# Placing the moving operands of a two-block transformer kernel: other start addresses for the second block's activations and products

## The reference

```python
def swiglu(x, w_gate, w_up, w_down):
    return (jax.nn.silu(x @ w_gate) * (x @ w_up)) @ w_down
...
    for l in range(DEPTH):
        h = rmsnorm(x, ffn1_norm[l])
        x = x + 0.5 * swiglu_2(h, ffn1_w_gate[l], ffn1_w_up[l], ffn1_w_down[l])
        h = rmsnorm(x, mix_norm[l])
        p = h @ w_in[l]
        ...
        y = jnp.concatenate([y_pool, y_four, y_attn], axis=-1) @ w_out[l]
        x = x + y
        h = rmsnorm(x, ffn2_norm[l])
        x = x + 0.5 * swiglu_2(h, ffn2_w_gate[l], ffn2_w_up[l], ffn2_w_down[l])
    return rmsnorm(x, final_norm)
```

## Time and profile before

| | |
|---|---|
| median of 3 runs | 1993.99 us (1993.69 to 1995.05) |
| the profiled execution | 1994.2 us, span of its instructions 1992.4 us |
| mean granted TensorE clock | 0.999 |
| PE busy | 1976.9 us, 99% of the span, 16,150 matmuls |
| DVE, ACT, POOL busy | 1429.0 us (72%), 1019.4 us (51%), 152.7 us (8%) |
| the three lines of `three` | 84% of the chain that ended last |

### The profile page before, as it was taken

The page is one execution under the profiler, slowest core; times in us unless marked ns, Lnnn a source line. Parts: engine busy times, 40 slices in busy tenths (PEclk is TensorE's granted clock), DMA queues, the critical chain, the costliest instruction groups (busy, mean ns, idle before and its releaser), DMA issues.

```text
span 1992.4 us, 42293 instructions
## 1 busy us (share of the span) xinstructions
PE 1976.9 (99%) x16150; PEld 1936.5 (97%) x16150; DVE 1429.0 (72%) x2593; ACT 1019.4 (51%) x1525; POOL 152.7 (8%) x192
## 2 busy tenths in 40 slices
PE   9999999999999999999999999999999999999998
PEld 9999989999999999899999999999999999999998
DVE  6774887886688769888868775667756775667763
ACT  4433686554455447765446444564444443555443
POOL 0001122000100011210010000010000000100000
PEclk9999999999999999999999999999999999999999
DMA  7454423545454544245554664335454555435554
GB/s 258 172 203 165 170 86 128 190 168 196 157 182 175 188 150 164 86 174 193 184 188 152 223 220 179 128 146 192 179 215 165 190 201 193 148 125 180 189 208 150
DMA packets 46830, 346.66 MB, mean 174 GB/s; under 512 B 5344, under 2 KB 6416, under 8 KB 9232
## 3 DMA queue, kind: packets, MB, share of 16 engines
q1 hardware_dynamic: 44416, 335.63, 46.5%
q0 software_dynamic: 2320, 9.74, 1.5%
HBM read 344.29 MB, written 1.07 MB: 173 GB/s over the span
## 4 chain that ended last, share of the span: by engine, by line
PE 88%; DVE 6%; ACT 2%; DVEq 1%; issue 1%; DMA 0%; ACTq 0%; POOL 0%; SPq 0%
PE ps L589 28%; PE ps L591 28%; PE ps L590 28%; DVE w_lo L1909 2%; ACT w_hi L1235 1%; DVE cst L2378 0%; DVE pj L2357 0%; PE ps L1135 0%; DVE pj L2354 0%; ACT scratch L1586 0%; PE ps L1100 0%; DVE scratch L2323 0%; DMA raw<-in_w_up 0%; PE ps L925 0%; PE ps L936 0%
## 5 line engine op out<-in xcount | busy, mean ns | idle before, releaser
L1909 DVE TENSOR_TENSOR w_lo<-raw,w_hi 128x1024 fp32r<-128x1024 f32 (+1 forms) x582 | 748.7, 1313 | 167.4 <-ACT w_hi L1235 165.4
L1235 ACT ACTIVATE w_hi<-raw 128x1024 fp32r<-128x1024 f32 (+1 forms) x582 | 634.9, 1121 | 140.4 <-PE ps L591 126.5
L589 PE MATMUL ps<-x_hi,w_lo 128*128 128x256 f32 (+3 forms) x2416 | 693.0, 287 | 2.7 <-DVE x_lo L1996 1.4
L591 PE MATMUL ps<-x_hi,w_hi 128*128 128x256 f32 (+3 forms) x2416 | 685.5, 284 | 0.0
L590 PE MATMUL ps<-x_lo,w_hi 128*128 128x256 f32 (+3 forms) x2416 | 680.6, 282 | 0.0
L589 PEld LDWEIGHTS ps<-x_hi,w_lo 128*128 128x128 f32 x2416 | 454.6, 188 | 11.1 <-issue 5.9
L590 PEld LDWEIGHTS ps<-x_lo,w_hi 128*128 128x128 f32 x2416 | 455.4, 188 | 0.8
L591 PEld LDWEIGHTS ps<-x_hi,w_hi 128*128 128x128 f32 x2416 | 454.4, 188 | 0.0
L589 PE MATMUL ps<-hid_hi,w_lo 128*128 128x256 f32 (+1 forms) x1536 | 435.5, 284 | 0.7 <-DVE hid_lo L2107 0.4
L590 PE MATMUL ps<-hid_lo,w_hi 128*128 128x256 f32 (+1 forms) x1536 | 434.0, 283 | 0.0
L591 PE MATMUL ps<-hid_hi,w_hi 128*128 128x256 f32 (+1 forms) x1536 | 433.4, 282 | 0.0
(11 more groups left out here) (330 smaller groups left out, 1538.9 us busy)
## 6 DMA issues: line engine op xcount, KB each, us to landing
raw<-in_w_up SPq DMA_DIRECT2D x176, 1024.0 KB, 4.8
raw<-in_w_down SPq DMA_DIRECT2D x64, 1408.0 KB, 6.0
raw<-in_w_in SPq DMA_DIRECT2D x36, 1024.0 KB, 4.8
raw<-in_w_out SPq DMA_DIRECT2D x16, 1024.0 KB, 4.9
cst<-row_copy POOLq DMA_DIRECT2D x2, 1088.0 KB, 8.6
raw<-in_w_up SPq DMA_DIRECT2D x4, 512.0 KB, 6.8
cst<-in_consts POOLq DMA_DIRECT2D x1, 1537.5 KB, 6.5
prm<-in_prm POOLq DMA_DIRECT2D x2, 690.0 KB, 7.5
```

Of the source, the lines that this page charges most:

```text
L589: mm(dst, w_lo[:, j, cols], xa, start=first, stop=False)
L591: return mm(dst, w_hi[:, j, cols], xa, start=False, stop=last)
L1235: fn(w_hi[:, j, c], raw[:, j, c], ACT.Copy).then_inc(hi_done, 1)
L1909: v.tensor_tensor(w_lo[:, j, c], raw[:, j, c], w_hi[:, j, c].bitcast(F32), ALU.subtract)\
```

## The change

In the second block each stage gets its own start and pitch. Stages are counted 3l, 3l+1, 3l+2 in layer l: first FFN, mixer with its input projection, second FFN. `X_LAYOUT` holds for each of the six stages the start word of x_hi, that of x_lo and the pitch; `HID_LAYOUT` holds the same for the products of layer 0's first FFN, layer 0's second, layer 1's first and layer 1's second. No instruction is added, taken away or moved to another engine; the operands of the matmuls, and of the ACT and DVE instructions that write these chunks, get other addresses.

```diff
+        X_LAYOUT = ((0, 0, T1), (16, 48, T2), (48, 80, T2), (112, 16, T2), (48, 16, T2), (112, 80, T2))
+        HID_LAYOUT = ((0, 0, T1), (80, 80, T2), (80, 112, T2), (64, 96, T2))
...
-        xt_hi, xt_lo = chunks(x_hi_all, KD, T2), chunks(x_lo_all, KD, T2)
+        stage = [-1]
...
-        hidt_hi, hidt_lo = chunks(hid_hi_all, NF, T2), chunks(hid_lo_all, NF, T2)
...
         def x_of(T):
-            return (xt_hi, xt_lo) if T == T2 else (x_hi, x_lo)
+            if T != T2:
+                return x_hi, x_lo
+            at_hi, at_lo, pitch = X_LAYOUT[stage[0]]
+            return chunks(x_hi_all[:, at_hi:], KD, pitch), chunks(x_lo_all[:, at_lo:], KD, pitch)
 
         def hid_of(T):
-            return (hidt_hi, hidt_lo) if T == T2 else (hid_hi, hid_lo)
+            if T != T2:
+                return hid_hi, hid_lo
+            at_hi, at_lo, pitch = HID_LAYOUT[stage[0] // 3 * 2 + (1 if stage[0] % 3 else 0)] if stage[0] >= 0 else (0, 0, T2)
+            return chunks(hid_hi_all[:, at_hi:], NF, pitch), chunks(hid_lo_all[:, at_lo:], NF, pitch)
```

More of the change, by code:

```diff
@@ L1195, in _ @@
                 mm(ps[:, 7, 0:T2], rstd[:, 0:P], rstd[:, 0:T2], start=True, stop=True)
+            stage[0] = -1
             for l in range(DEPTH):
@@ L1211, in _ @@
                 t0, q, e0, r0 = l * TURNS2 + BLOCK2_TURN, l * 2 + 2 * DEPTH, l * 4 + EVENT2, l * 3 + 3 * DEPTH
+                stage[0] = 3 * l
                 if l == 0:
@@ L1219, in _ @@
                 pe.wait_ge(consts_in, 16 * (1 + len(CONST_PARTS)))
+                stage[0] = 3 * l + 1
                 pieces = mixer2(l, t0 + SEC2["in"], e0 + 1, l * 3 + 1)
+                stage[0] = 3 * l + 2
                 out_proj(t0 + SEC2["out"], e0 + 2, r0 + 1, T2, (cat_hi2, cat_lo2), OUT2_BANK, pieces, CAT_ORDER)
@@ L1887, in _ @@
                 if l < DEPTH - 1:
+                    stage[0] = 3 * l + 3
                     down(t0 + SEC2["ffn2"] + UP_T, r0 + 2, True, s0 + 2, T2, "nextg")
```

## The result

The change makes the kernel slower. Median 2004.56 us (2004.39 to 2006.17, 5 runs) against 1993.88 us (1993.26 to 1995.05, 5 runs) of the kernel before beside it: +10.7 us, ratio 1.0058 with a 95% interval of 1.0046 to 1.0069. The forecast of 1989 us and its range up to 1997 us were wrong; the rival on the other side, "agreement is the collision", had 2004 us.

The account below looks back on a forecast made before the run. PE's matmul count times start-to-start spacing was taken as the bound. Terms -3.9 + 0 - 1.0 + 0.1 + 0.6 = -4.2 us, rounded to -5, against the 1993.99 us median gave 1989 us; range 1976 to 1997 us.

Parts of the forecast that it names:

- agreement is the collision: Rival: moving chunk and weight block starting on the same residue collide; typically +10 us, 2004 us; chance 0.13.
- That PE's spacing bounds the kernel: Second block: matmul count times start-to-start distance sets the time; PE waits 0.6 us from 1346 to 1922 us.
- That placement sets the pace: Moving operand and next weight load hold each other up by addresses repeating with 256 bytes; 10 to 12 ns surplus per matmul.
- the rival "nothing": Rival: placement does not set the pace, or all residues are passed anyway; 1994 us, within 2 us; chance 0.25.
- Part 1: x at 0/0, three up projections and layer 1's mixer: 3552 matmuls from 117.8 to 116.7 ns, -3.9 us.
- Part 2: Layer 0's mixer at 128/128: 384 matmuls, 0, between -1.5 and +2.1 us.
- Part 3: Second block's first up projection, chunks 272 words apart: 960 matmuls from 118.9 to 117.9 ns, -1.0 us.
- Part 4: Second block's first down projection, same 272-word walk: 528 matmuls, 117.6 to 117.9 ns, +0.1 us.
- Part 5: Other three down projections, at 64/192, 64/64, 0/0: 1584 matmuls at 116.6 ns; +0.6 us, all from the first.
- the lower rival: Rival: stretches settle lower than any now, all matmuls at 114 ns; some -17 us, 1977 us; chance 0.17.

Follow-up runs that it names:

- The map: Table of paces by hi and lo distance, from two kernels changing only second-block start words (1996.4 and 1996.8 us), the kernels before and after, and partial reversals.
- s1: The changed kernel with only the start words in the layout tables altered, another pair of distances per second-block stage; 1996.4 us, one run.
- k1: b2 with the first of the eight chunks of x apart from the others, at 0/0 instead of 192/192; 1971.19 us, ratio to before 0.9886.
- b1: Second block's up, down and input projections all at 192/192, pitch 256, against the kernel before; 1988.97 us, ratio 0.9981.
- b2: As b1, with the concatenated heads of the second block's output projections also at 192/192; 1974.22 us, ratio to before 0.9921.

## Why the prediction was wrong

**That PE's spacing bounds the kernel, and that the change acts through nothing else**, held: same waits, same busy times of DVE and ACT, the whole 10.7 us in the pace.

**That placement sets the pace**, against the Trainium skill's rule and the rival "nothing", held as well, and more than I had read: 113.3 to 121.1 ns for one instruction. The Trainium skill (TensorE: Matmul & The Clock Gate, Step-by-step: what each phase is for) has the running matmul undisturbed by the next weight load. No run here shows the reads themselves. What they show is that moving only the weights (c2) changes the pace of matmuls whose moving operand did not move, and that moving both together (c1) changes nothing; that fits two reads that get in each other's way, and doesn't fit the rule. The prediction also used the formula of the Trainium skill (TensorE: Matmul & The Clock Gate, Back-to-back issue gap), 109.2 ns. That section gives it for an isolated gap, and says that in a stream of weight loads and matmuls both set the spacing. So it speaks neither for nor against placement that no stretch reached the figure (the best pace here is 113.3 ns).

**Part 1 failed**, and decided the sign. It priced x at 0/0 at 116.7 ns, -3.9 us; measured 120.0 (119.8 in layer 1's mixer), and these stages are 7.1 us longer. The choice between the bounds of 114 and 123.3 ns rested on one sentence: in the earlier trace rows the chunk at distance 0 isn't a slow one. But there hid_lo is at 128, and the chunk is 272 columns wide. The map says that a pair is not the sum of its parts: hi at 0 goes with 120.0, 117.8 or 116.7 by where lo is, and hi at 192 with 113.3 to 119.2. One part's distance, read from a walk over pairs, said nothing about another pair. The other reason, that two unlike layouts had come out at 116.7, was no reason for a third. The nearest honest statement was that 0/0 lay between the bounds with no lean, which would have given both signs like chances instead of 0.62 to 0.13.

**Part 2** (128/128, 0) was mis-sized by 0.3 us: the mixer went from 117.8 to 118.6 ns, and a down projection at 128/128 (s1) at 118.7.

**Part 3** (-1.0) came to 0. The 118.9 ns that it started from the earlier trace rows aren't all spacing: in that row PE is busy 89.40 of 90 us. At the one pause two starts come 0.88 and 0.22 us behind the one before, 0.9 us too much together, 1.1 ns per matmul. The pace inside it was 117.8 already, as in the other stages, and the walk has 117.8 too. The busy column stood beside the count, and I didn't use it. **Part 4** (+0.1) held.

**Part 5** (+0.6) was +2.9: the stage at 64/192 went to 117.8 as said (+0.6), 64/64 as well (+0.6 for 0), and 0/0, "even by part 1", to 120.0 (+1.8).

**The rival** "agreement is the collision" gave 120.0 ns for part 1 and 2004 us for the whole, both as measured. That the whole fits is in part luck: its sum at 120.0 ns was +7.5 us, rounded up to +10, and most of the rest came from part 3's missing gain and from the down projections at 64/192 and 64/64. Its mechanism is not shown either: 192/192 and 64/64 agree too, and are fast and middling. Distance 0/0 is slow, and the map doesn't say why. Nor was the remark against the lower rival right, that a fast start is always paid for by a slow one next to it: at 192/192 all of them are fast for a thousand matmuls on end.

What stays open: the rule behind the map, and what in the start behind a pause picks the pace. Whether the first block, with 258 to 274 columns, gains in the same way wasn't tried.

## What to carry to other kernels

Where PE is busy all the time and its matmuls start further apart than their columns need, try the start addresses of the moving operand relative to the weights, modulo 256 bytes: it costs no instruction, and here the span from worst to best was 7%. Try pairs as a whole on the chip, in one kernel with another layout per stage, since neither part alone nor a neighbour 32 or 64 bytes off tells the value. And look at several executions: a layout may have two paces, taken where PE pauses, so that a single trace shows one of them and a median of few runs is partly luck.

## What the runs showed of the hardware that I had not expected

- The pace of identical matmuls (256 columns, clock 1.00) ranges from 113.3 to 121.1 ns with the addresses alone.
- While the distances stay, it is kept for as long as PE doesn't pause: at 192/192 either 113.3 or 117.8 ns, through an up projection and the down projection behind it (1488 matmuls). Three matmuls at another distance left it as it was at 160 of 161 places in k1, though only four of these came in at the slow pace.
- Executions of one program differ by it: in steps of 6.6 us in b1, by up to 22 us in b2, where the kernel before stays within 4.2 us over all its 50 runs.
- Which pace follows a pause repeats with the place in the program: 21 of 22 entries in the mixers are alike in b1 and b2. The long loops differ between executions, and what decides there isn't known.
